# One tile in two of a mixture-of-experts weight stream, issued by GpSimd instead of SyncE

## The chip, the cores and the metric

One core of a Trainium2 chip runs the whole program. The metric is the device time of one execution in microseconds; the figure for a kernel is the median of its runs.

## The reference

Two transformer layers of different build follow each other on x, 512 tokens of 1024 features, in float32: first a layer with an RWKV branch, a dilated attention and a mixture of experts, then two layers with sparse and banded attention and a gated feed-forward. The change touches the mixture of experts alone:

```python
def expert_block(args):
    xblk, e = args
    return (jax.nn.silu(xblk @ w_gate[e]) * (xblk @ w_up[e])) @ w_down[e]
```

There are 32 experts; each token goes to its two best within its best group of eight. `w_gate` and `w_up` of an expert are 1024x512, `w_down` is 512x1024: 2 MB each (2.10 million bytes), 96 matrices, 201 million bytes in all, each read once.

## The kernel before, in words

The program writes each engine's instructions out by hand, with semaphores between them: `tensor_program`, `vector_program`, `scalar_program`, `pool_program` (GpSimd, "POOL" in the profile) and `sync_program` (SyncE, "SP"). A wait `wait_ge(*at(label))` holds the instructions behind it on its own engine alone.

**The expert stage.** The experts are worked in 16 pairs, called experts j = 0 to 15 in what follows. Each of a pair's two experts has 64 slots for tokens (`SLOTS`); the two halves of 128 rows go through PE side by side, h = 0 and h = 1 (`HP[h]`). A pair has six weight tiles of 2 MB, numbered i = 6j to 6j + 5: gate h = 0, gate h = 1, up h = 0, up h = 1, down h = 0, down h = 1. Even numbers belong to the first expert of the pair, odd ones to the second. Tile i lies in `wslot[i % 8]`, so eight tiles have room at a time.

**PE** (line 1380 `expert_up`, line 1401 `expert_down`) waits for both tiles of a kind (`expert_in`) and then runs the product: gate, up, transposes of the next pair's tokens (`expert_in`, line 1356), and down. Between them it scatters the pair before into the rows of the result. At the end of the gate product it signals `gu, j, 0`, at the end of up `gu, j, 1`, of down `y, j, 1`.

**SP** (line 3114 `expert_tile`) issues all weight tiles in order on its own hardware queue, q1 in the profile. Tile i waits until the tile eight before it has been used:

```python
if i >= 8:
    jb, pb = (i - 8) // 6, (i - 8) % 6 // 2
    sp.wait_ge(*(at("gu", jb, pb) if pb < 2 else at("y", jb, 1)))
```

Tiles 0 to 7 are loaded ahead of the stage, 8 and 9 in two halves each (`second_halves`), 10 to 95 in the loop at line 3172. Behind them SP waits for the last up product (`gu, 15, 1`) and loads the first tiles of the second block, into buffers that overlap the experts' ones.

**POOL** (line 3046) issues on the software queue, q0, one gather for each expert j from 1 on: an indirect DMA that brings the 128 token rows of 4 KB (0.5 MB) into `Gt[j % 2]`. Gather j waits until PE has transposed the tokens of expert j - 2 (`xt, j - 2, 1`). PE wants gather j in `expert_in(j)`, between the up and down products of expert j - 1. Otherwise POOL has nothing to do in the stage; afterwards it waits for `y, 15, 1`.

The stage ends with the down product of expert 15, the scatter of its eight parts and the additions to X; the norm of the second block needs all of X.

Of the kernel before, what the change touches and what calls it, by code (L numbers as in the profile page):

```python
# [82 lines left out]
class Marks:  # L83
# [18 lines left out]
    def landed(self, name, *label):  # L102
        return self.up(name, *label, by=16)
# [5 lines left out]
    def at(self, *label):  # L109
        if not self.known:  # L110
            return None, 0
        name, value = self.known[label]
        return self.handle(name), value
# [24 lines left out]
class Engine:  # L138
# [50 lines left out]
    def max(self, *a, **k):  # L189
        return self.e.max(*a, **k)  # L190
# [42 lines left out]
def program(nc, T, out):  # L233
    ctx = ExitStack()
    marks = Marks(nc, ctx)
    up, landed, also, at, now = marks.up, marks.landed, marks.also, marks.at, marks.now
# [5 lines left out]
    def sb(name, lo, *shape, dt=F32):  # L242
        n = int(np.prod(shape))
        words = n if dt is not BF16 else n // 2
        assert lo >= 0 and lo + words <= TOP, (name, lo, words)
        assert dt is not F32R or lo % 16 == 0, name
        t = nc.alloc_sbuf_tensor_at(name, [128, n], dt, offset=BASE + 4 * lo)
        return shaped(t[:, :], shape)
# [92 lines left out]
    for L in range(2):  # L341
# [13 lines left out]
        part = []  # L355
        for k0, chs in zip((0, 12), FF):
            ups = [(c0, w, [chunks_of(wgu, [(u * 2816 + c0, w)])[0] for u in range(2)]) for c0, w in chs]
            nk = sum(w for _, w in chs) // 128
# [94 lines left out]
    wslot = [sb(f"wslot{i}", lo, 4096) for i, lo in enumerate(W_AT)]  # L453
# [2545 lines left out]
    def pool_program(po):  # L2999
# [43 lines left out]
        po.dma_start(t_pi, T["pos2"]).then_inc(*landed("pos2", "t2", "pos_in"))  # L3043
        po.wait_ge(*at("rows"))
        po.wait_ge(*at("logits"))
        for j in range(1, 16):
            po.wait_ge(*at("srow", int(j >= SLOT_PARTS[0][1])))
            if j != 2:
                po.wait_ge(*at("xt", max(j - 2, 0), 1))
            po.indirect_dma_start(out=Gt[j % 2], out_offset=None, in_=rows,  # L3050
                                  in_offset=bass.IndirectOffsetOnAxis(ap=srow[:, j:j + 1],
                                                                      axis=0)).then_inc(*landed(f"gather{j % 2}",
                                                                                                "gathered", j))
        po.wait_ge(*at("y", 15, 1))
        po.wait_ge(*at("flag"))
        known = dict(po.seen)
# [46 lines left out]
    def sync_program(sp):  # L3103
# [10 lines left out]
        def expert_tile(i):  # L3114
            j, part, h = i // 6, i % 6 // 2, i % 2
            src = T[("w_gate", "w_up", "w_down")[part]][0, 2 * j + h]
            nk = (8, 8, 4)[part]
            dst, src = wslot[i % 8].rearrange("p (k n) -> p k n", k=nk), src.rearrange("(p k) n -> p k n", p=128)
            if i in (8, 9):
                sp.wait_ge(*at("gate_half"))  # L3120
                sp.dma_start(dst[:, 0:4, :], src[:, 0:4, :]).then_inc(*landed(f"wslot{i % 8}"))
                return
# [3 lines that stand above are left out]
            elif i == 7:  # L3126
                sp.wait_ge(*at("logits"))
            sp.dma_start(dst, src).then_inc(*landed(f"wslot{i % 8}", "expert_in", i))

        def second_halves():  # L3130

            sp.wait_ge(*at("gu", 0, 0))
            for i in (8, 9):
                dst = wslot[i % 8].rearrange("p (k n) -> p k n", k=8)
                src = T["w_up"][0, i - 6].rearrange("(p k) n -> p k n", p=128)
                sp.dma_start(dst[:, 4:8, :], src[:, 4:8, :]).then_inc(*landed(f"wslot{i % 8}", "expert_in", i))
# [32 lines left out]
        for i in range(7, 10):  # L3169
            expert_tile(i)  # L3170
        second_halves()
        for i in range(10, 96):
            expert_tile(i)

        sp.wait_ge(*at("gu", 15, 1))
# [4 lines left out]
        with sp.branch(flag[0:1, 0:1]):  # L3180
            sp.wait_ge(*at("y", 15, 1))
            for x in range(32):
                for n, name in enumerate(("w_gate", "w_up", "w_down")):
                    if x:
                        sp.wait_ge(*(at("f_gu", 4 * x - 1, 1) if n < 2 else at("f_y", 8 * x - 1)))
                    nk = (8, 8, 4)[n]
                    sp.dma_start(wslot[F_SLOTS[n]].rearrange("p (k n) -> p k n", k=nk),
                                 T[name][0, x].rearrange("(k p) n -> p k n",
                                                         p=128)).then_inc(*landed(f"f_w{n}", "f_in", 3 * x + n))
# [9 lines left out]
    def write_out(engines):  # L3199
        tensor_program(engines[0])  # L3200
        vector_program(engines[1])
        scalar_program(engines[2])
        pool_program(engines[3])
        sync_program(engines[4])
# [3 lines left out]
    with ctx:  # L3208
        block = ctx.enter_context(nc.Block())

        @block.tensor
        def _(e):
            tensor_program(Engine(e))

        @block.vector
        def _(e):
            vector_program(Engine(e))

        @block.scalar
        def _(e):  # L3220
            scalar_program(Engine(e))

        @block.gpsimd
        def _(e):
            pool_program(Engine(e))

        @block.sync
        def _(e):
            sync_program(Engine(e))
# [50 lines left out]
```

## Time and profile before

| | |
|---|---|
| median of 3 runs | 2903.51 us (2901.78 to 2904.3) |
| profiled execution, its own time | 2900.81 us |
| its span, first to last instruction | 2898.9 us |
| mean granted TensorE clock | 0.976 |
| PE busy | 2733.8 us (94%) |
| DVE, ACT, POOL busy | 1596.7, 907.3, 136.1 us |
| DMA moved | 475.68 MB, 164 GB/s over the span |
| q1 (hardware, SP) | 367.62 MB |
| q0 (software, POOL) | 86.63 MB |
| expert stage, weight tiles under way without a break | about 830 to 1270 us |

The times of the views count from the start of the span. PE's busy share can't be read as PE at its peak, since the ends of matmuls are modelled. The DMA share is the mean over the core's 16 DMA engines. "To landing" is the time from the issue of a DMA to its semaphore. A bracket behind a row gives the idle time of its engine before it and what ended that.

### The profile page before, as it was taken

The numbers are of one execution on the slowest core, as the hardware profiler recorded it, in microseconds if no ns is written. First come the engines' busy times: TensorE is split into PE (matmuls) and PEld (weight loads), VectorE is DVE, ScalarE is ACT, GpSimd is POOL, SyncE is SP. The second block draws the span as 40 slices with busy tenths as digits, with TensorE's granted clock in tenths as the row PEclk, the third lists the DMA queues.
The fourth block names the chain that finished last, engine by engine and source line by source line (L and its number), as shares of the span: only waits on it lengthen the run. The fifth ranks groups of instructions, "written<-read, shape, count | busy, mean of one in ns | idle before, by whom it ended". The sixth has DMA issues, their size and how long they took to land.

```text
span 2898.9 us, 46763 instructions
## 1 busy us (share of the span) xinstructions
PE 2733.8 (94%) x20088; PEld 2028.9 (70%) x20088; DVE 1596.7 (55%) x2982; ACT 907.3 (31%) x1492; POOL 136.1 (5%) x236
## 2 busy tenths in 40 slices
PE   7999999998899999989999999999999999999999
PEld 5777777887643333338677778888786777788887
DVE  4675666765543333345676556665456765543343
ACT  5323232316410100022345533223223455332221
POOL 0010101010000000000000000000000000000000
PEclk9999999999999999989999999999999999999999
DMA  4232333254499999963253326664232442233332
GB/s 153 74 115 94 102 93 111 89 176 176 185 377 427 427 427 427 428 244 96 69 115 122 113 81 189 190 194 146 84 86 73 117 128 84 87 95 99 98 95 80
DMA packets 149926, 475.68 MB, mean 164 GB/s; under 512 B 13632, under 2 KB 40880, under 8 KB 137168
## 3 DMA queue, kind: packets, MB, share of 16 engines
q1 hardware_dynamic: 114688, 367.62, 35.4%
q0 software_dynamic: 24944, 86.63, 9.4%
q10 hardware_dynamic: 10080, 18.35, 2.2%
q8 instruction: 161, 2.64, 0.4%
q14 instruction: 53, 0.43, 0.0%
HBM read 451.05 MB, written 21.51 MB: 163 GB/s over the span
## 4 chain that ended last, share of the span: by engine, by line
PE 80%; DMA 9%; DVE 7%; ACT 3%; issue 2%; POOL 0%; SPq 0%; DVEq 0%; ACTq 0%; POOLq 0%
PE psum L154 76%; DMA wslot<-in_w_gate 4%; PE psum L157 3%; DMA wslot<-in_w_up 3%; DVE slot L163 1%; DVE n_ht L166 1%; DVE halfL L163 1%; DVE m_acc L169 1%; DMA m_in<-in_w_ada 0%; DVE X L163 0%; DVE hL L163 0%; DMA colb<-in_cols 0%; DVE sc__240 L169 0%; ACT halfH L160 0%; DVE gx L163 0%
## 5 line engine op out<-in xcount | busy, mean ns | idle before, releaser
L163 DVE TENSOR_TENSOR halfL<-ring,halfH 128x1024 fp32r<-128x1024 f32 x302 | 368.1, 1221 | 535.7 <-ACT halfH L160 535.2
L160 ACT ACTIVATE halfH<-ring 128x1024 fp32r<-128x1024 f32 x302 | 317.3, 1053 | 731.4 <-PE psum L154 720.3
L154 PE MATMUL psum<-hH,halfH 128*128 128x512 f32 x1200 | 484.2, 404 | 8.2 <-DVE hL L163 4.2
L154 PE MATMUL psum<-hL,halfH 128*128 128x512 f32 x1200 | 470.6, 392 | 0.0
L154 PE MATMUL psum<-hH,halfL 128*128 128x512 f32 x1200 | 470.5, 392 | 0.0
L154 PEld LDWEIGHTS psum<-hH,halfH 128*128 128x128 f32 x1200 | 226.4, 189 | 83.7 <-issue 30.4
L154 PE MATMUL psum<-wslot,XT 128*64 128x512 f32 x1024 | 236.3, 604 | 27.6 <-DMA wslot<-in_w_gate 22.5
L154 PEld LDWEIGHTS psum<-hH,halfL 128*128 128x128 f32 x1200 | 226.8, 189 | 48.7
L154 PEld LDWEIGHTS psum<-hL,halfH 128*128 128x128 f32 x1200 | 226.9, 189 | 43.1
L154 PE MATMUL psum<-halfH,hH 128*128 128x512 f32 (+2 forms) x576 | 226.2, 393 | 23.7 <-DVE hL L163 11.3
L154 PE MATMUL psum<-halfL,hH 128*128 128x512 f32 (+2 forms) x576 | 215.1, 373 | 0.0
L154 PE MATMUL psum<-halfH,hL 128*128 128x512 f32 (+2 forms) x576 | 214.6, 373 | 0.0
L154 PEld LDWEIGHTS psum<-wslot,XT 128*64 128x64 f32 x1024 | 73.4, 138 | 166.3 <-issue 164.5
L163 DVE TENSOR_TENSOR X<-X,psum 128x512 f32<-128x512 f32 x136 | 88.4, 683 | 132.9 <-PE psum L154 129.7
L154 PEld LDWEIGHTS psum<-halfH,hH 128*128 128x128 f32 x576 | 115.2, 200 | 54.0 <-issue 27.6
L154 PEld LDWEIGHTS psum<-slot,slot 64*64 64x64 f32 x4096 | 126.0, 136 | 29.6 <-issue 11.7
L154 PE MATMUL psum<-slot,slot 64*64 64x64 f32 x4096 | 134.4, 221 | 12.2 <-DVE slot L163 7.1
L154 PE MATMUL psum<-halfH,aH 128*128 128x512 f32 x352 | 136.9, 389 | 0.0
L154 PE MATMUL psum<-halfL,aH 128*128 128x512 f32 x352 | 136.9, 389 | 0.0
L154 PE MATMUL psum<-halfH,aL 128*128 128x512 f32 x352 | 136.9, 389 | 0.0
L154 PEld LDWEIGHTS psum<-halfH,hL 128*128 128x128 f32 x576 | 115.4, 200 | 17.7
L154 PEld LDWEIGHTS psum<-halfL,hH 128*128 128x128 f32 x576 | 115.8, 201 | 14.8
(482 smaller groups left out, 4135.7 us busy)
## 6 DMA issues: line engine op xcount, KB each, us to landing
wslot<-in_w_gate SPq DMA_DIRECT2D x32, 2048.0 KB, 26.7
wslot<-in_w_down SPq DMA_DIRECT2D x32, 2048.0 KB, 27.0
ring<-in_w_in SPq DMA_DIRECT2D x120, 512.0 KB, 3.7
wslot<-in_w_up SPq DMA_DIRECT2D x30, 2048.0 KB, 27.0
ring<-in_w_gu SPq DMA_DIRECT2D x88, 512.0 KB, 3.6
m_in<-in_w_ada POOLq DMA_DIRECT2D x96, 256.0 KB, 3.1
m_in<-in_w_ada POOLq DMA_DIRECT2D x48, 512.0 KB, 4.8
ring<-in_w_down SPq DMA_DIRECT2D x44, 512.0 KB, 3.5
```

What stands on the lines that cost most here:

```text
L154: return self.e.matmul(*a, **k)
L157: return self.e.transpose(*a, **k)
L160: return self.e.activation(*a, **k)
L163: return self.e.tensor_tensor(*a, **k)
L166: return self.e.tensor_scalar(*a, **k)
L169: return self.e.scalar_tensor_tensor(*a, **k)
```

## The change

From tile 16 on, SP issues the even tiles alone. POOL issues the odd ones, 17 to 95, with the same destination, source and condition, on q0, between its gathers: for each p, the tiles 6p + 9 (an up tile) and 6p + 11 (a down tile), then gather p + 3, then tile 6p + 13 (a gate tile). The odd tiles have semaphores of their own (`pslot`), and the label PE waits for stays the same. Bytes, buffers and all arithmetic stay as they are.

```diff
         po.wait_ge(*at("rows"))
         po.wait_ge(*at("logits"))
-        for j in range(1, 16):
+        def gather(j):
             po.wait_ge(*at("srow", int(j >= SLOT_PARTS[0][1])))
             if j != 2:
                 po.wait_ge(*at("xt", max(j - 2, 0), 1))
...
+        def odd_tile(i):
+            part = i % 6 // 2
+            jb, pb = (i - 8) // 6, (i - 8) % 6 // 2
+            nk = (8, 8, 4)[part]
+            po.wait_ge(*(at("gu", jb, pb) if pb < 2 else at("y", jb, 1)))
+            po.dma_start(wslot[i % 8].rearrange("p (k n) -> p k n", k=nk),
+                         T[("w_gate", "w_up", "w_down")[part]][0, 2 * (i // 6) + 1].rearrange("(p k) n -> p k n", p=128)
+                         ).then_inc(*landed(f"pslot{i % 8}", "expert_in", i))
+
+        gather(1)
+        gather(2)
+        for p in range(15):
+            for i in (6 * p + 9, 6 * p + 11):
+                if 16 <= i < 96:
+                    odd_tile(i)
+            if p + 3 < 16:
+                gather(p + 3)
+            if 16 <= 6 * p + 13 < 96:
+                odd_tile(6 * p + 13)
         po.wait_ge(*at("y", 15, 1))
...
         second_halves()
-        for i in range(10, 96):
+        for i in [*range(10, 16), *range(16, 96, 2)]:
             expert_tile(i)
```

## Rows read from the trace of the kernel before

**Rows 1.** The page's slices: DMA share in tenths, and GB/s, 40 slices of 72.5 us.
```profile
DMA  4232333254499999963253326664232442233332
GB/s 153 74 115 94 102 93 111 89 176 176 185 377 427 427 427 427 428 244 96 69 115 122 113 81 189 190 194 146 84 86 73 117 128 84 87 95 99 98 95 80
```

**Rows 2.** Windows of the expert stage: length, busy time by engine, granted clock, DMA.
```profile
core 0: us, PE busy (x) PEld busy (x) DVE busy (x) ACT busy (x) POOL busy (x), PEclk, DMA share, GB/s
850.00:875.00 25.00, 24.78 (x118) 9.79 (x118) 9.24 (x16) 2.57 (x4) 0.94 (x1) 1.00 1.01 425
...
1100.00:1125.00 25.00, 24.24 (x104) 9.88 (x106) 8.10 (x13) 1.20 (x2) 0.94 (x1) 0.93 1.01 428
1150.00:1175.00 25.00, 22.09 (x94) 8.47 (x95) 7.71 (x13) 2.57 (x4) 0.94 (x1) 0.93 1.01 427
1221.80:1251.20 29.40, 27.43 (x124) 10.93 (x125) 9.63 (x16) 2.57 (x4) 0.00 (x0) 1.00 1.01 429
```

**Rows 3.** Timeline of POOL: start, us, the gather, idle time before it.
```profile
909.86 0.94 POOL L199 DMA_INDIRECT Gt<-h_rows,srow  x1 [26.45 <-PE psum L157]
...
1057.22 0.94 POOL L199 DMA_INDIRECT Gt<-h_rows,srow  x1 [29.71 <-PE psum L157]
```

**Rows 4.** The chain that ended last, longest pieces: start, us, what.
```profile
1066.07 34.33 DMA wslot<-in_w_gate
...
1191.56 30.16 DMA wslot<-in_w_gate
```

**Rows 5.** PE's waits, 965 to 1268 us: total, times, longest.
```profile
PE psum L154 <- DMA wslot<-in_w_gate: 22.5, 10, 4.0
```

**Rows 6.** Timeline of PE: products of experts 12, 14 and 15.
```profile
1161.83 5.35 PE L154 MATMUL psum<-wslot,XT 128*64 128x512 f32 x16 [2.69 <-DMA wslot<-in_w_gate]
...
1221.85 3.65 PE L154 MATMUL psum<-wslot,XT 128*64 128x512 f32 x16 [1.42 <-DMA wslot<-in_w_gate]
...
1251.22 3.65 PE L154 MATMUL psum<-wslot,XT 128*64 128x512 f32 x16 [1.41 <-DMA wslot<-in_w_gate]
...
1271.67 7.09 PE L154 MATMUL psum<-wslot,aT 128*64 128x512 f32 x32 [0.22 <-ACT aT L160]
```

**Rows 7.** SP's issues of tiles 90, 91 and of 94, 95, with time to landing.
```profile
L196 SPq DMA_DIRECT2D wslot<-in_w_gate x2: 328/380/432, 1220.5 to 1220.8; - x2
DMA to landing us min/median/max: 25.7/28.0/30.2
...
L196 SPq DMA_DIRECT2D wslot<-in_w_down x2: 328/380/433, 1240.1 to 1240.4; - x2
DMA to landing us min/median/max: 25.7/27.9/30.2
```

**Rows 8.** Timeline of POOL: its last plain load before the stage.
```profile
779.35 0.56 POOL L196 DMA_DIRECT2D t_pi<-in_pos  x1 [124.30 <-PE psum L154]
```

**Rows 9.** POOL's gathers, 850 to 1250 us: idle before them, time to landing.
```profile
  PE psum L157: 343.9, 12
...
DMA to landing us min/median/max: 10.7/11.0/11.3
```

**Rows 10.** DMA packets of 1240 to 1250 us, and of q0 from 0.5 to 12 us.
```profile
DMA packets 297, 4.33 MB, mean 433 GB/s; under 512 B 33, under 2 KB 33, under 8 KB 33
...
q0 software_dynamic: 290, 1.42, 34.4%
```

**Rows 11.** DMA queues while a gather runs, 1155 to 1160 us: packets, MB, share.
```profile
q1 hardware_dynamic: 109, 1.62, 76.6%
q0 software_dynamic: 114, 0.47, 22.9%
```

**Rows 12.** DMA queues while X and others load, 653 to 670 us.
```profile
q0 software_dynamic: 1463, 5.55, 86.2%
```

## The prediction

> **What bounds the kernel now.** I looked first at the page's slices, because the moved transfers belong to one stretch. Slices 12 to 17 have the DMA at 9 and 427 GB/s [rows 1]; that is the expert stage. The windows of that stage [rows 2] show two regimes. Until about 960 us PE is busy 24.8 of 25 us and the DMA is full as well: the eight weight buffers were filled early, and that stock is being eaten up. An expert then costs 27.4 us, the distance of the gathers that GpSimd issues (26.45 idle and 0.94 for the issue [rows 3]). From about 965 us the stock is gone. The gathers are 29.71 + 0.94 = 30.65 us apart, and the longest pieces of the chain of waits are landings of expert tiles, of some 30 us each [rows 4]. So the stage goes at PE's pace up to 965 us and at the pace of the bytes after it: six tiles of 2.10 MB and a gather of 0.52 MB are 13.11 MB, and 13.11 MB in 30.65 us are 427.7 GB/s. PE's waits for gate tiles are short but regular, 22.5 us in 10 waits [rows 5].
>
> The end of the stage decides here. Expert 14 starts its gate product at 1221.85, expert 15 at 1251.22, and its down product ends at 1271.67 + 7.09 = 1278.76 [rows 6]. Expert 15 thus takes 27.54 us after its first tiles are in, PE's own pace with no large wait in it. Its gate tiles (90 and 91 of the 96) are issued at 1220.47 and 1220.8, and land after 25.7 and 30.2 us, the second at 1251.0. The down tiles (94, 95) are issued at 1240.05 and 1240.4 and land at 1265.8 and 1270.6 [rows 7]. The last byte is there 1.1 us before PE wants it. **Two limits meet here**: the last byte, and the landing of tile 91 plus 27.5 us of PE work. FIFO order gives tile 91 a distance of 1270.6 - 1251.0 = 19.6 us, four tiles of 4.9 us, to the last byte.
>
> **The change, part by part.** Bytes, buffers and waits stay. Tiles 17, 19, ... 95, 40 of them and 83.9 MB, go from q1 to q0; tiles 16, 18, ... 94 stay.
>
> *Issuing.* SP loses 40 issues of 0.38 us [rows 7], POOL gains 40 of about 0.56 us (the price of its last plain load before the stage [rows 8]), 22 us in all. POOL waits for 343.9 us in this stage [rows 9], and SP for slots: both cost nothing. On POOL each odd tile waits for what it waited for on SP (end of gate, of up, of down), in the order in which PE produces these, and the gather's wait (PE's transposes) lies between up and down. Nobody is held by an order that is wrong.
>
> *Gather.* It lands 11.0 us after issue now [rows 9]. Behind two or three queued odd tiles it may take 30. Gather j is issued when expert j-2's tokens are transposed, and wanted two experts, 59 us, later. Cost nothing; its cover would be gone only at twice the 30 us.
>
> *Rate.* In the last expert period, without a gather, the engines move 429 GB/s at a share of 1.01 [rows 2]: they are full with one queue, and a second cannot add. Its packets: from 1240 to 1250 us there are 297, 33 of them under 512 B, for 4.33 MB, so 264 of 16.4 KB, one per partition row [rows 10]. The instruction is the same on POOL, so I take the same packet for q0. At the start q0 moved 290 packets for 1.42 MB, 4.9 KB each on average [rows 10], so its packets are not held to 4 KB. Cost 0, with the smaller packet as a rival.
>
> *Order of landing.* This is the term that counts. While a gather runs beside q1, q0 has 114 packets and q1 109, though q0 moves 0.47 MB and q1 1.62 [rows 11]: the engines take the queues in turn, packet by packet. With 16 KB packets on both, each queue gets half of 427 GB/s, and a tile takes 9.8 us instead of 4.9. If the two queues stayed level, tiles 2m and 2m+1 would both land when the later one lands today, and since PE waits for both halves before a product, nothing would be lost. They do not stay level. Per expert q0 carries 6.29 + 0.52 MB, q1 6.29. Tile 17 has a small lead, for it passes what SP queued before it; one or two gathers use that up, and a dozen more at 1.2 us each (2.5 us where the rate is shared) put q0 behind. Once q1 has run dry it stays so: a new even tile finds its queue empty and takes every second packet, while the odd one waits behind two or three others. Even tiles then lie in their buffers and wait for partners.
>
> In the middle this costs nothing: as long as an odd tile is queued the engines are full, PE gets a pair per 9.8 us in either order, and the last byte lands at 1270.6 as before. At the end it does. I follow the queue. When the last pair is issued (end of expert 14's up product), q0 holds 91, 93, 95; q1 holds 94 and, before it, r tiles (a rest of 92, or 92 and 90). Today 30.2 us of work are outstanding there (6 tiles and 1 us of latency). If PE is late by x, then x less is left: (29.2 - x) / 4.9 = 3 + 1 + r. With r = 0, x = 9.6; with r = 2 (level queues) x = 0. So tile 91 is late by 0 to 9.6 us. The odd tiles land in an uneven beat, since a tile on q0 gets half the engines or all of them as q1 is busy or dry; followed back over the last experts with gate 9.4, up 8.3, 2.7 between and down 7.1 us, r comes out near 0.3. Then x = 29.2 - 21.1 = 8.1 us. I take **+8 us**; PE then needs its 27.5 us regardless of how early 94 and 95 are, and every later stage, the next loads of SP among them (issued at that up product's end), moves by the same amount.
>
> *Clock.* Waits before a gate product are 2.7 us each now and will be 0 to 6 us in turn. Of the present ten two fall together with a granted clock of 0.93 in their window [rows 2]; at one of them 16 matmuls take 5.35 us instead of 3.65 [rows 6]. In the middle this hides in the wait; on the last expert it would cost 1.7 us. I count 0 and keep 1.7 for the range.
>
> Sum: 0 + 0 + 0 + 8 = +8 us. Against the profiled execution's 2900.8 us (span 2898.9) that gives 2908.8; the median of the runs is 2903.5, 2.7 us above it, so 2911.5. A measurement of this kernel can tell about 0.2%, 5.8 us, from no change.
>
> **Rivals.**
> 1. *Level queues, no change.* Each tile's partner lands within 2 us, and tile 91 is late by 0 to 2 us: 2903.5 to 2905.5. For it: in both queues the same number of tiles of the same size, released together. Against: the gathers' extra 0.52 MB per expert, and nothing that pulls a late queue forward. The Trainium skill (DMA: Bandwidth & Descriptors, "Issuing engines are not separate DMA queues") says that issuing from several engines only saves the sequencer's time; by that rule the result is this one, about 2903.5. The gather that shares packet by packet [rows 11] says that such transfers also trade places, which the rule doesn't price. Chance 0.27.
> 2. *Small packets on q0, clearly slower.* If GpSimd cuts a row into 4 KB, the nearest price is the gather's: the period with it is 30.65 us, without it 29.37 [rows 3, 6], so 0.52 MB cost 1.28 us, 2.44 us per MB beside the tiles' 29.37 / 12.58 = 2.33. On 83.9 MB that is +9 us, and q1 with four times the bytes per turn runs dry at once, so x = 9.6: together some +19, 2922.5. Upwards it may go further: the 2 MB load of X and its neighbours ran at 5.55 MB in 86.2% of 17 us, 379 GB/s [rows 12], which would make the rate's part 83.9 x (2.64 - 2.33) = +26. For it: nearly all of q0's packets now are of 4 KB. Against: the 4.9 KB average [rows 10]. The same page ("SWDGE vs HWDGE vs iDMA") says a software packet has 4096 B or less "preferably"; by that alone the sum would be this rival's. Chance 0.12.
> 3. *Faster.* The queues' turns close small gaps between q1's tiles, and the stage, bound by bytes from 965 to 1251 us, runs at the 433 GB/s that a 10 us stretch shows [rows 10] instead of 427.7: 1.3% of 286 us, -3.6, and with the PE-bound part's stock eaten more slowly at most -6: 2897.5. It decides only if gate 15 starts earlier than 1251.2, so the lag must stay under 3 us too. PE's floor would allow it. Against: a DMA share of 1.01, no gap to close. Chance 0.07.
>
> **How the numbers follow.** The lag has 0.54, of which 0.48 lie over 5.8 us and 0.06 under. Slower by over 0.2%: 0.48 + 0.12 + 0.02 of rival 1 with a slow clock = 0.62. Within: 0.06 + 0.25 + 0.01 = 0.32. Faster: 0.06. The forecast is that of the lag. Its own range is 2908 to 2915 (x of 4.5 to 9.6, and 1.7 for the clock). The 8 in 10 take in level queues at the lower end, down to 2902.5, and the lower part of rival 2 at the upper, 2921; what is left out is rival 3 and most of rival 2.
>
> **What would show it.** Right: q0 with 83.9 MB more, DMA at 427 GB/s to the same time (about 1265), odd tiles landing 5 to 20 us after their even partners from about 930 us on, waits before gate products of uneven length (0 and 6 us), even ones short to land and odd ones long, gate 15 starting at 1257 to 1261, the y product's end as much later, and the stages behind it unchanged in length. Wrong: pairs landing within 2 us and gate 15 at 1251 (rival 1); q0 packets of 4 KB and a lower rate in the stage (rival 2); the stage's rate over 430 and gate 15 before 1250 (rival 3); or a change in the second block, where nothing is moved.

## The result, and the profile after

The changed kernel takes 2912.75 us (median of 15 runs, 2904.72 to 2916.7); the kernel before took 2903.33 us in the 15 runs beside it (2900.6 to 2906.89). The medians differ by 9.4 us. The ratio, taken over all runs, is 1.0026, with a 95% interval of 1.0018 to 1.0034, which is 7.5 us (5.2 to 9.9). In a second series it was 1.0038, 1.0024 to 1.0053. The forecast was 2911.5.

The profiled execution took 2914.91 us, its span is 2912.8. The page's slices and queues, to be held beside [rows 1]:

```profile
DMA  4232323254499999952244225664222442233332
GB/s 152 74 114 84 111 89 113 89 180 170 185 378 426 427 427 427 427 229 79 79 115 128 98 87 180 192 195 149 91 78 80 115 128 84 87 94 95 101 94 80
...
q1 hardware_dynamic: 108928, 283.73, 28.5%
q0 software_dynamic: 30704, 170.52, 16.2%
```

The queues have exchanged 83.9 MB, and q0 has 5760 packets more: 40 tiles of 144, that is 128 data packets of 16 KB and 16 small ones each, as on q1. The stage runs at 427 GB/s as before.

Windows of the stage (length, busy time by engine, granted clock, DMA share, GB/s) show that the bytes come at the old pace and PE takes them unevenly:

```profile
950.00:975.00 25.00, 18.70 (x76) 6.55 (x74) 5.21 (x8) 4.20 (x6) 1.09 (x2) 0.86 1.01 427
975.00:1000.00 25.00, 24.78 (x117) 9.55 (x114) 8.33 (x13) 2.57 (x4) 2.58 (x4) 1.00 1.00 427
...
1200.00:1225.00 25.00, 21.73 (x91) 8.95 (x92) 6.48 (x11) 0.61 (x2) 1.06 (x2) 0.86 1.01 429
```

From one stretch of 25 us to the next PE is busy for 18.7 and 24.8 us; the kernel before had 22.9 and 23.1 in the same two. The DMA share is 1.01 or 1.00 throughout. Landing times of the odd tiles (first line) and of the even ones (second) between 965 and 1250 us say why:

```profile
DMA to landing us min/median/max: 25.0/29.1/34.4
...
DMA to landing us min/median/max: 13.3/14.2/17.0
```

Both tiles of a pair are issued within 0.3 us of each other. The even one is there after 14 us and waits 15 us for the odd one. A gather behind the odd tiles lands after 33 us and no longer 11 [rows 9]; nobody waits for it. The chain of waits, longest pieces, answers to [rows 4]. There landings of some 30 us stood at irregular places; here a landing and a stretch of PE work follow each other in turn:

```profile
1048.44 32.15 DMA wslot<-in_w_gate
1080.72 19.47 PE psum L154 x76
1110.31 30.97 DMA wslot<-in_w_gate
1141.41 19.52 PE psum L154 x76
1171.03 32.11 DMA wslot<-in_w_gate
1203.28 19.65 PE psum L154 x76
1233.03 29.13 DMA wslot<-in_w_gate
```

The pieces come every 61 to 62 us, two experts: a beat of two, in which each second gate product waits and the other finds its tiles.

The end of the stage, PE's timeline (start, us, product), to be held beside [rows 6]:

```profile
1232.92 3.65 PE L154 MATMUL psum<-wslot,XT 128*64 128x512 f32 x16 [0.20 <-DMA wslot<-in_w_gate]
...
1262.29 3.65 PE L154 MATMUL psum<-wslot,XT 128*64 128x512 f32 x16 [1.42 <-DMA wslot<-in_w_gate]
...
1282.41 7.09 PE L154 MATMUL psum<-wslot,aT 128*64 128x512 f32 x32 [0.22 <-ACT aT L160]
```

and the landings of tile 91 (POOL, issued at 1233.0), 94 (SP, 1251.1) and 95 (POOL, 1251.4), beside [rows 7]:

```profile
L196 POOL DMA_DIRECT2D wslot<-in_w_gate x1: 531/531/531, 1233.0 to 1233.0; - x1
...
DMA to landing us min/median/max: 29.1/29.1/29.1
...
L196 SPq DMA_DIRECT2D wslot<-in_w_down x1: 328/328/328, 1251.1 to 1251.1; - x1
DMA to landing us min/median/max: 17.0/17.0/17.0
...
L196 POOL DMA_DIRECT2D wslot<-in_w_down x1: 531/531/531, 1251.4 to 1251.4; - x1
DMA to landing us min/median/max: 22.4/22.4/22.4
```

To compare traces, I count from the start of the first gather, which lies at 808.11 us before and at 811.51 here:

| from the first gather, us | before | changed |
|---|---|---|
| gate 15 starts | 443.1 | 450.8 |
| last weight byte landed | 462.5 | 462.2 |
| down 15 ends | 470.7 | 478.0 |

The bytes end on time, PE 7.3 us late. Tile 91 lands 11.6 us before the last byte, not 19.6. It is not the only thing that is late: gate 15 waits 1.42 us for it, so with tile 91 on time PE would still have started gate 15 some 6.3 us late, because of its wait at gate 13 (run 3 below). Of the 13.9 us between the two spans 3.4 lie ahead of the first gather and 3.2 behind the stage, where nothing was changed. Across all eleven traces the part ahead took 803.5 to 812.8 us and the part behind 1620.1 to 1625.1; the kernel before, traced a second time, had 1625.1 behind. Those two parts are the spread from run to run, not the change.

### The profile page after: what moved, and what is told of

Read it like the earlier page. It is cut to its first block, busy times and chain, and to the rows that moved or that the text cites. A ratio compares the mean times of both kernels' runs of the same rounds, so it can differ in the third digit from the quotient of the medians.

```text
span 2912.8 us, 46763 instructions
## 1 busy us (share of the span) xinstructions
PE 2740.3 (94%) x20088; PEld 2028.4 (70%) x20088; DVE 1597.1 (55%) x2982; ACT 907.3 (31%) x1492; POOL 158.4 (5%) x276
## 4 chain that ended last, share of the span: by engine, by line
PE 80%; DMA 8%; DVE 7%; ACT 3%; issue 2%; POOL 0%; ACTq 0%; DVEq 0%; POOLq 0%
PE psum L154 77%; DMA wslot<-in_w_gate 7%; PE psum L157 3%; DMA m_in<-in_w_ada 1%; DVE slot L163 1%; DVE m_acc L169 1%; DVE n_ht L166 1%; DVE halfL L163 0%; DVE X L163 0%; DVE hL L163 0%; ACT halfH L160 0%; DMA brow<-in_b_in 0%; DMA colb<-in_cols 0%; DVE sc__240 L169 0%; DVE gx L163 0%
## 5 line engine op out<-in xcount | busy, mean ns | idle before, releaser
L154 PE MATMUL psum<-hH,halfL 128*128 128x512 f32 x1200 | 470.7, 392 | 0.0
```

Source lines behind the costliest of these rows:

```text
L154: return self.e.matmul(*a, **k)
```

## The experiments

Theory A is the forecast's: what counts is how late the last expert's gate pair (90, 91) lands before the last byte. Theory B is a cost of the software queue by itself (rate, issue), theory C a cause outside the stage. Each experiment was run beside the kernel before (median 2902.2 us in both series).

**1. The changed kernel once more.** 

> The changed kernel, unaltered, once more. Theory A (the end of the stage is late because tile 91, an odd gate tile, lands late): +8 to +10 us to before again, and in the new trace gate 15 starts 6 to 10 us later, counted from the first gather, than the 443.1 us of before; the last weight byte lands at the same distance, 462.5 us. Theory B (the odd tiles cost bandwidth or issue time on the software queue): the last byte too is late by as much. Theory C (the difference lies outside the stage, and the first trace was one draw): the stage has the length of before in this trace.

2912.17 us, ratio 1.0038 (1.0024 to 1.0053). In this trace gate 15 starts 449.4 us after the first gather and down 15 ends at 476.6, while the last byte is there at 460.9. Its span was only 2903.4 us, because the part ahead took 805.0: single executions hide the effect, the stage counted from the gather doesn't. Gate 15 is late by 6.3 us, the lower part of what A said, and here it waits only 0.17 us for a tile. The last byte comes no later than before, so B falls, and the stage is longer than before, so C falls.

**2. Software queue up to tile 77 only.**
```diff
-        for i in [*range(10, 16), *range(16, 96, 2)]:
+        for i in [*range(10, 16), *range(16, 78, 2), *range(78, 96)]:
```
and POOL's conditions end at 78 as well. 

> Tiles 17 to 77 odd stay on the software queue; from 78 on (experts 13, 14, 15) SP issues all. 31 of the 40 moved tiles are still moved. Theory A: by expert 15 the queues are one again, tile 91 has four whole tiles behind it, so gate 15 starts at 443 to 444 us from the first gather and the time is that of before within 2 us (2903 to 2905). Theory B: 31/40 of the loss stays, +7 us. Theory C: +8 to +10 as in the changed kernel or nothing to do with it.

2903.87 us, ratio 1.0006 (0.9995 to 1.0016). 31 tiles still go by q0, and the loss is gone. The end of the stage is that of before: the first gather is at 809.91, so gate 15 starts at 442.2 and down 15 ends at 469.8.

```profile
1252.14 3.65 PE L154 MATMUL psum<-wslot,XT 128*64 128x512 f32 x16 [0.28 <-DMA wslot<-in_w_gate]
...
1272.58 7.09 PE L154 MATMUL psum<-wslot,aT 128*64 128x512 f32 x32 [0.22 <-ACT aT L160]
```

Delay in the middle of a stage that the bytes bound is given back, if the order is restored early enough; B's +7 is excluded by the interval, whose upper end is 4.6 us.

**3. Only the last three odd tiles back on SP** (78 above replaced by 90). 

> Only 91, 93 and 95 go back to SP; 17 to 89 odd stay on the software queue. Theory A in a simple form (only the last expert's own three odd tiles count): back to before, 2903 to 2905. Theory A in full (the odd down tile 89 and the tiles before it are still behind when the last expert's are issued, so the last expert can't start on time however its own tiles are sent): still +5 to +7 us, 2909 to 2911. Theory B: +9.

2907.55 us, ratio 1.0017 (1.0006 to 1.0028), +5.3 us: the full form. The trace shows a step that my sum had left out. Neither gate 14 nor gate 15 waits for a tile any more; gates 14 and 15 follow each other at PE's pace:

```profile
1197.26 5.35 PE L154 MATMUL psum<-wslot,XT 128*64 128x512 f32 x16 [3.85 <-DMA wslot<-in_w_gate]
...
1226.37 3.60 PE L154 MATMUL psum<-wslot,XT 128*64 128x512 f32 x16
...
1253.73 3.60 PE L154 MATMUL psum<-wslot,XT 128*64 128x512 f32 x16
...
1273.78 7.09 PE L154 MATMUL psum<-wslot,aT 128*64 128x512 f32 x32 [0.22 <-ACT aT L160]
```

The last wait is the first line's, 3.85 us at gate 13, for the odd tile 79, which landed at 1197.1, 391.9 us after the gather (gate 13 before: 384.2). From there PE has no wait for a tile left to make up with. Behind that wait the 16 matmuls take 5.35 us and not 3.65, at a granted clock of 0.68, which adds 1.7 us. Before, an expert takes 29.4 us at the end and PE alone needs 27.4, so a delay shrinks by 2 us per expert at most: 7.9 us at the start of gate 13, 1.7 more in it, then 7.4 at gate 14, 5.4 at gate 15 and 5.0 at the end of down 15. That also is why going back at 78 helps and at 90 doesn't: 79 is among the tiles that have to be in order.

**4. The odd tiles on ScalarE's hardware queue.** `odd_tile` stands in `scalar_program`: 6j + 9 and 6j + 11 behind the sigmoid of expert j, 6j + 13 behind its two output copies; POOL keeps the gathers alone.
```diff
+                odd_tile(6 * j + 9)
+                odd_tile(6 * j + 11)
...
+                odd_tile(6 * j + 13)
```


> The odd tiles 17 to 95 are issued by ScalarE on its hardware queue, with the same conditions; the gathers stay alone on the software queue. Theory A1 (the gathers, which share the odd tiles' queue, push these back): the two tile queues carry the same bytes, pairs land within some 2 us of each other, and the time is that of before within 2 us. Theory A2 (any two queues that are served in turn let one run ahead, here the one that gets its first tile at once past a queued backlog): a lag remains, even or odd, followed about half as large, +3 to +5 us, 2906 to 2908. Theory B: nothing is on the software queue, so 2903.5.

2904.24 us, ratio 1.001 (1.0001 to 1.0018), +2.0 us. Landings of three pairs each between 1170 and 1230 us, SP's first, ScalarE's second:

```profile
DMA to landing us min/median/max: 27.9/29.1/32.5
...
DMA to landing us min/median/max: 23.9/25.1/28.5
```

The partners are 4 us apart, not 15, and with a steady sign: SP's, which had the backlog when the second queue opened, is the later one. Gate 15 starts 3.4 us late, down 15 ends 3.1 us late. So it lies between A1 and A2: most of the lag goes when the gathers leave the odd tiles' queue, and a remainder of 3 to 4 us stays. By its sign it belongs to the start; no run opened both queues level, so that is argued, not shown. A gather, now one of three queues taken in turn, lands after 15.8 us.

**5 and 6. Both kernels without gathers.** The gathers of experts 3 to 15 are left out of the kernel before (5) and of the changed one (6).
```diff
-            pe.wait_ge(*at("gathered", j))
+            pe.wait_ge(*at("gathered", 2 - j % 2))
```
with `range(1, 3)` for the gathers in 5, and `gather(p + 3)` left out in 6. 

> The kernel before, with the gathers of experts 3 to 15 left out (13 of 15; their tokens are then those of experts 1 and 2). It is the base for the next run. 13 x 0.52 MB are 6.8 MB less in a stage that the bytes bound, at 1.28 us for each gather 16.6 us; the 4 or 5 in the part that goes at PE's pace only lengthen that part, which comes to the same sum. Theory: 2902.2 - 16 = 2886.

> The changed kernel with the same gathers left out: the two tile queues carry the same bytes and nothing else. Theory A1 (the gathers in the odd tiles' queue make the lag): pairs land within 2 us of each other, and the time is within 2 us of the run before without gathers, some 2887. Theory A2 (two queues served in turn drift apart by themselves): +7 to +10 us to that run, 2894 to 2896, odd tiles 10 to 20 us behind even ones as in the changed kernel. Theory B (the software queue costs by itself): +9.

5: 2887.66 us, against 2886 expected, ratio to the kernel before 0.9946 (0.9929 to 0.9963). 6: 2889.51 us, 0.9948 (0.9931 to 0.9965). With the same 40 tiles on q0 the medians differ by 1.9 us. Four runs each leave some 5 us open on either side, so the traces have to decide: gate 15 starts 3.3 us later in 6 than in 5 (428.5 and 425.2 from the gather), against 7.7 us with gathers. Queues of run 6 from 830 to 1240 us:

```profile
q1 hardware_dynamic: 6322, 92.06, 53.0%
q0 software_dynamic: 5708, 82.24, 47.2%
```

92.06 MB for 53.0% and 82.24 for 47.2% are 1.737 and 1.742 MB per point: a byte costs the same on either queue, and q0's packets average 14.4 KB with the small ones counted, like q1's 14.6. That ends theory B and the small packets. Landings of the pairs issued between 1170 and 1222 us, SP then POOL:

```profile
DMA to landing us min/median/max: 30.5/30.7/30.7
...
DMA to landing us min/median/max: 27.7/27.9/27.9
```

Without gathers the odd tile is the earlier one, by 2.5 us once its later issue is taken off (A1 had said 2), and it stays at that through the last experts. Tile 90, the even one, is what gate 15 starts with: it lands at 1235.0. The two queues don't drift apart by themselves (A2); what pushes q0 back by 15 us are the gathers (A1).

**7. Only tiles 91, 93 and 95 on the software queue.**
```diff
-        for i in [*range(10, 16), *range(16, 96, 2)]:
+        for i in [*range(10, 90), *range(90, 96, 2)]:
```
and POOL from 90 on. 

> Only tiles 91, 93 and 95 go to the software queue; SP issues the other 37. Theory A says that not the number of moved tiles counts but what lands in front of the last gate pair: the three find an empty queue, take every second packet from the four or five tiles queued on q1, and land early (within some 10 us of issue), while 90 on q1 gets half the rate and has only 92 and 94 behind it. It lands 9.8 us before the last byte and not 19.6: gate 15 starts 9 to 10 us late, +8 to +10 us, 2911 to 2912, though a thirteenth of the tiles is moved. Theory B (a cost per moved tile): 3/40 of 10 us, +0.7.

2910.87 us, ratio 1.0027 (1.0016 to 1.0038): +8.7 us with three tiles moved, nearly as much as with forty. Tile 90 (SP) and tile 91 (POOL), both issued at about 1226.4 us:

```profile
DMA to landing us min/median/max: 37.8/37.8/37.8
...
DMA to landing us min/median/max: 14.5/14.5/14.5
```

The last byte lands at 1273.8 (tile 94, issued at 1249.2, after 24.6 us), tile 90 at 1264.1, 9.7 us before it. The same loss with the other sign: here the odd tile has overtaken and the even one is late. The tiles of expert 14 on q1 are held up as well, and PE waits for them:

```profile
1239.14 5.32 PE L154 MATMUL psum<-wslot,XT 128*64 128x512 f32 x16 [3.65 <-DMA wslot<-in_w_up]
...
1255.03 8.79 PE L154 MATMUL psum<-wslot,aT 128*64 128x512 f32 x32 [3.37 <-DMA wslot<-in_w_down]
```

So PE reaches gate 15 only 0.5 us before tile 90 lands; either delay alone would have cost almost the whole 8.4 us by which gate 15 is late.

**8. Forty tiles on q0, and a bound on q1's lead.**
```diff
+            if i >= 24:
+                sp.wait_ge(*at("expert_in", i - 3))
```
in SP's `expert_tile`, behind its present wait. 

> All 40 odd tiles stay on the software queue; SP waits, from tile 24 on, before it issues even tile i until odd tile i - 3 has landed, so that q1 can't run ahead by more than a pair. Theory A: the engines stay full (q0 has work while SP waits), the lag at the end shrinks from about 8 to some 3 us, by hand tile 91 lands 3 us late: +2 to +4 us, 2904.5 to 2906. Theory B, and any theory in which the added wait only costs: +9 or more.

2905.91 us, ratio 1.0016 (1.0004 to 1.0028), +3.7 us: a wait was added, and 6 us of the loss are gone. In the trace down 15 still ends 4.8 us late. Tile 91 is not the reason: I had said 3 us late, and it lands 0.9 us late, 443.8 us from the gather, while gate 15 starts at 448.3 without waiting for a tile. Gate 14 starts 4.2 us late, and behind its wait of 3.06 us the granted clock is 0.50 for the first 2.7 us of the product, the lower of the two levels (1.2 GHz):

```profile
1225.27 6.59 PE L154 MATMUL psum<-wslot,XT 128*64 128x512 f32 x16 [3.06 <-DMA wslot<-in_w_gate]
...
1255.64 3.60 PE L154 MATMUL psum<-wslot,XT 128*64 128x512 f32 x16
```

6.59 us in place of 3.65, behind the last wait, so 2.9 us that nothing gives back.

**9. The kernel before, a second trace.** 

> The kernel before, unaltered, for a second trace of it. Theory A: the last weight byte lands 462 us and the last down product ends 470.7 us after the first gather, within 1 us, as in its first trace. What lies ahead of the stage and behind it may differ by some us from run to run (ahead 803 to 812 us, behind 1620 to 1625 in the traces so far); if the part behind it is again near 1620, and all the altered kernels show 1622 to 1625, something is carried over the end of the stage beyond the delay itself.

One execution, span 2904.6 us: the first gather at 809.38, the last byte at 462.0, the end of down 15 at 470.1 us from it, the part behind at 1625.1. The stage repeats within 0.6 us; the 5 us behind it vary from run to run in one and the same kernel, and nothing shows that a delay is carried over.

All together, with the end of down 15 counted from the first gather (before 470.7 and 470.1), and the medians to 2902.2 (for 6, to run 5):

| kernel | end of down 15 | later by | median later by |
|---|---|---|---|
| changed, two traces | 478.0, 476.6 | 7.3, 5.9 | 10.0 |
| 2, q0 up to tile 77 | 469.8 | -0.9 | 1.7 |
| 3, q0 up to tile 89 | 475.7 | 5.0 | 5.3 |
| 4, ScalarE's queue | 473.8 | 3.1 | 2.0 |
| 6 to 5, no gathers | 455.9 to 452.7 | 3.1 | 1.9 |
| 7, last three on q0 | 478.7 | 8.0 | 8.7 |
| 8, bounded lead | 475.4 | 4.8 | 3.7 |

Six of the seven rows agree within 2.6 us. For the changed kernel the median says 10.0 (9.4 in the first series) and two traces 7.3 and 5.9. The ratio of the first series, 7.5 us, fits the traces; that of the second, 7.0 to 15.4 us, only the larger of them. Whether other runs have a larger lag (the prediction's count allows 9.6 us) two traces can't settle. No version with all its gathers is faster than the kernel before; its last down product starts 1.1 us after the last byte, and another order of landing has no more than that to gain.

## Why the prediction was right

**Issuing and the gather's cover**, both taken at nothing: right. POOL issues a tile in 0.53 to 0.57 us and idles before each; the gathers took 33 us to land, against "it may take 30", and none was waited for.

**Rate**, taken at nothing: right. 427 GB/s before and after, and the price per byte in run 6 is the same for both queues. That q0's packets aren't cut to 4 KB, inferred from an average of 4.9 KB, held: 144 packets for a tile, as on q1.

**Order of landing**, +8 us: right in mechanism and size. The last byte came at 462.2 against 462.5 us, gate 15 was later by 7.7 us (at 1262.3 from the start of the span, where 1257 to 1261 had been said; the part ahead was 3.4 us longer), and tile 91 landed 11.6 us before the last byte, so x was 19.6 - 11.6 = 8.0 against 8.1. That closeness is partly luck: r of 0.3 was followed back, and in the second trace of the same kernel gate 15 was 6.3 us late. The cause named in it, the gathers on the odd tiles' queue, is shown by runs 5 and 6. What the step lacked: it treated level queues as harmless in any order of opening. Run 7 shows a second way to the same loss, and run 4 points to it by its sign. A queue that opens beside a backlog overtakes it, and run 7 pays 8.7 us for three tiles. The other gap is that the delay need not come from the last gate at all. Run 3 takes it from gate 13, and in the changed kernel that path is only 1.4 us shorter than the one by tile 91.

**Clock**, 0 with 1.7 us for the range: right for the changed kernel, since gate 15 waited only 1.42 us and took 3.65 us. The term asked only about the last expert; in runs 3 and 8 the slow product was gate 13's and gate 14's, and its 1.7 and 2.9 us were never given back. Its premise of waits of 2.7 us each was read too evenly: half of the ten are near that, the others are 1.1 to 1.4 us and 4.0.

**Rivals.** Level queues come near being true without gathers only: partners 2.5 us apart in run 6, and down 15 still 3.1 us late. The Trainium skill's rule (DMA: Bandwidth & Descriptors, "Issuing engines are not separate DMA queues"), that issuing from several engines saves the sequencer's time and no more, agrees with run 6 on the rate, 1.9 us from run 5; runs 7 and 1 show what it doesn't say, that splitting an ordered stream changes its order, at 8.7 and 10 us. The Trainium skill also says (DMA: Bandwidth & Descriptors, "Queues, rings and completion order") that each DMA engine takes the rings in turn, packet by packet; the changed kernel's trace agrees, with 113 packets on each queue from 1142 to 1150 us and 180 and 173 from 1234 to 1246 us. Neither small packets nor a higher rate came: from 970 to 1215 us the stage moved 427 GB/s before and after.

The waits before gate products alternated as foreseen up to gate 14: none or 0.2 us, then 4.05 to 6.30 us.

## What to carry to other kernels

Where bytes bound a stage, the DMA share can stay full and the last byte on time whatever the order of the transfers (here 460.9 to 463.3 us from the first gather in all nine traces with gathers); look instead at how long before the last byte each tile of the last round lands, and add the work that follows it. A stream whose consumer needs it in order should stay on one queue, or be split only where both queues carry equal bytes and start level, which no run here did in full; a small transfer on one of them (here 0.5 MB beside 6.3) is enough to put its tiles behind by several tiles, and a queue opened beside a backlog overtakes it. A delay ahead of the last rounds is given back only as fast as the consumer is faster than the stream, 2 us per expert here.

## What the runs showed of the hardware that was not expected

The granted clock fell at nearly all of the long waits. In the changed kernel's first trace PE waited 4.05 to 6.30 us before each second gate product between 950 and 1210 us, and the 16 matmuls behind took 5.34 to 5.50 us, five times of five. Three of them:

```profile
957.69 5.41 PE L154 MATMUL psum<-wslot,XT 128*64 128x512 f32 x16 [6.30 <-DMA wslot<-in_w_gate]
1018.82 5.35 PE L154 MATMUL psum<-wslot,XT 128*64 128x512 f32 x16 [4.39 <-DMA wslot<-in_w_gate]
1080.72 5.34 PE L154 MATMUL psum<-wslot,XT 128*64 128x512 f32 x16 [5.23 <-DMA wslot<-in_w_gate]
```

At the first of these products the granted clock was 0.50, the lower of its two levels (1.2 GHz), from 955.0 us on, while PE still waited, and up to 961.0. Before, with waits of 2.7 us, the 16 matmuls took 3.65 at 976.40, 1007.06 and 1068.34; they took 5.35 twice, at 1161.83 behind 2.69 us [rows 6] and at 1100.53 behind 3.99 us. It isn't a fixed rule of the wait's length: in run 1 they took 6.42, 6.33 and 5.69 us behind waits of 3.59, 3.91 and 5.16 us, but 3.65 behind one of 3.66 us. Few long waits can so cost more PE time than many short ones of the same sum. From 965 us on there were 22.5 us in 10 waits before [rows 5] and 20.5 in 6 after, and the slow products behind them added 3.4 us before and 6.9 after. In the middle of the stage the next wait absorbs that; behind the last wait it stays.

And the second queue's depth shows in a gather's landing: 11.0 us beside one deep queue, 15.8 beside two, 33 behind the tiles of its own.
